# Order of the two heads of a pair in the matmuls of an RWKV-7 layer

## What is computed

```python
sa = einsum('bhij,bhj->bhi', s, at)
s = s * wt + sa[..., None] * bt + vt[..., None] * kt
y = einsum('bhij,bhj->bhi', s, rt)
```

## Time and profile before

| what | value |
|---|---|
| executions | 3149.65, 3150.62, 3152.99 us |
| span of the profiled execution (its own time; no other is given) | 3154.0 us |
| PE matmul busy | 2964.0 us (94%), 24726 instructions |
| PE weight load busy | 2386.1 us (76%) |
| DVE, ACT, POOL busy | 1796.9, 1140.6, 300.5 us |
| the slots of the RWKV layer | about 1140 to 1625 us |

### The profile page before, as it was taken

The page is one execution under the profiler, slowest core; times in us unless marked ns, Lnnn a source line. Parts: engine busy times, 40 slices in busy tenths (PEclk is TensorE's granted clock), DMA queues, the critical chain, the costliest instruction groups (busy, mean ns, idle before and its releaser), DMA issues. The chain is left out here.

```text
span 3154.0 us, 55883 instructions
## 1 busy us (share of the span) xinstructions
PE 2964.0 (94%) x24726; PEld 2386.1 (76%) x24726; DVE 1796.9 (57%) x2769; ACT 1140.6 (36%) x1779; POOL 300.5 (10%) x390
## 2 busy tenths in 40 slices
PE   7999998899998988898989999999899999999999
PEld 3775535899985468888949989876799897455898
DVE  3348566756554067778736555467555554465553
ACT  2236402434331234344223343444543433144432
POOL 2222011000000013323210000000000000200000
PEclk9999999999999999999989999999999999999999
DMA  7323544355543010000035545543355554423353
GB/s 263 104 107 107 187 149 146 117 188 192 191 172 120 27 28 3 3 3 3 32 132 177 190 161 179 180 156 134 100 168 181 165 178 174 139 75 132 109 187 134
DMA packets 258170, 409.33 MB, mean 130 GB/s; under 512 B 18647, under 2 KB 111208, under 8 KB 257800
## 3 DMA queue, kind: packets, MB, share of 16 engines
q1 hardware_dynamic: 253832, 392.50, 36.2%
q0 software_dynamic: 4096, 13.25, 1.5%
HBM read 400.68 MB, written 2.95 MB: 128 GB/s over the span
## 5 line engine op out<-in xcount | busy, mean ns | idle before, releaser
L353 DVE TENSOR_TENSOR ring_parts<-ring,arena_parts 128x2048 fp32r<-128x2048 f32 x270 | 598.4, 2256 | 285.7 <-ACT arena_parts L346 283.2
L346 ACT CAST arena_parts<-ring 128x2048 fp32r<-128x2048 f32 x270 | 495.4, 1885 | 517.1 <-PE psum L2822 229.5
L2822 PE MATMUL psum<-arena_parts 128*128 128x256 f32 x2816 | 514.6, 286 | 3.1 <-DVE arena_parts L578 2.1
L2822 PEld LDWEIGHTS psum<-arena_parts 128*128 128x128 f32 x2816 | 445.3, 195 | 4.2 <-DVE arena_parts L578 3.0
L2822 PE MATMUL psum<-arena_parts,ring_parts 128*128 128x256 f32 x1408 | 401.7, 285 | 0.0
L390 PE MATMUL psum<-arena_parts 128*128 128x512 f32 x1024 | 327.0, 393 | 2.0 <-DVE arena_parts L578 2.0
L2822 PEld LDWEIGHTS psum<-arena_parts,ring_parts 128*128 128x128 f32 x1408 | 274.0, 195 | 0.0
L1855 PE MATMUL psum<-arena_parts 128*128 128x512 f32 x768 | 236.6, 389 | 0.0
L390 PEld LDWEIGHTS psum<-arena_parts 128*128 128x128 f32 x1024 | 193.8, 190 | 43.0 <-DVE arena_parts L578 2.7
L390 PE MATMUL psum<-ring_parts,arena_parts 128*128 128x512 f32 x560 | 219.5, 392 | 0.0
L1840 PE MATMUL psum<-arena_parts 128*128 128x256 f32 x896 | 163.3, 285 | 4.2 <-DVE ring_parts L353 4.0
(11 more groups left out here) (498 smaller groups left out, 5888.1 us busy)
## 6 DMA issues: line engine op xcount, KB each, us to landing
ring<-in_mlp_w SPq DMA_DIRECT2D x48, 2048.0 KB, 8.2
ring<-in_ada_w SPq DMA_DIRECT2D x24, 2048.0 KB, 7.8
ring<-in_ffn_pre_w_gu SPq DMA_DIRECT2D x44, 1024.0 KB, 6.6
ring<-in_ffn_post_w_gu SPq DMA_DIRECT2D x44, 1024.0 KB, 7.1
ring<-in_ffn_pre_w_down SPq DMA_DIRECT2D x8, 2048.0 KB, 7.8
ring<-in_xmem_wkv SPq DMA_DIRECT2D x8, 2048.0 KB, 8.0
ring<-in_ffn_post_w_down SPq DMA_DIRECT2D x8, 2048.0 KB, 7.7
ring<-in_ab_w_in SPq DMA_DIRECT2D x7, 2048.0 KB, 7.7
```

Of the source, the lines that this page charges most:

```text
L346: nc.scalar.copy(high_view(name)[:, k, :], raw_view(name)[:, k, :]).then_inc(*up(act, ("high", name, h)))
L353: nc.vector.tensor_tensor(low_view(name)[:, k, :], raw_view(name)[:, k, :], high_view(name).bitcast(F32)[:, k, :], ALU.subtract)\
L2822: ins = nc.tensor.matmul(psum[:, b, 256 * j:256 * j + 256], s[:, k, at:at + P], x_parts[q][:, k, :], start=(k == 0 and i == 0), stop=(k == ...
```

## The change

Only the order of matmuls on PE changes, in three functions; shapes, banks, waits and counts stay.

```diff
             gram_pe, for f, z, c in gram_at(f, tick)
                 for r in HH:
                     k_, b_ = Kh[f % 2][z][r, s], Bh[f % 2][z][r, s]
                     if c < 4:
                         nc.tensor.matmul(psum[r, b, 0:64], b_, R_[f % 3][z][r, c, :], start=True, stop=True)
-                        nc.tensor.matmul(psum[r, b, 64:192].rearrange("p (a t) -> p a t", a=2), k_,
-                                         RA[f % 3][z][r, :, c, :], start=True, stop=True)
                     else:
                         nc.tensor.matmul(psum[r, b, 128:192], k_, A_[f % 3][z][r, c, :], start=True, stop=True)
-                    nc.tensor.matmul(psum[r, b, 192:256], b_, cst("eye64")[r, :], start=True, stop=True)
-                    ins = nc.tensor.matmul(psum[r, b, 256:320], k_, cst("eye64")[r, :], start=True, stop=True)
+                if c < 4:
+                    for r in HH:
+                        nc.tensor.matmul(psum[r, b, 64:192].rearrange("p (a t) -> p a t", a=2), Kh[f % 2][z][r, s],
+                                         RA[f % 3][z][r, :, c, :], start=True, stop=True)
+                for r in HH:
+                    nc.tensor.matmul(psum[r, b, 192:256], Bh[f % 2][z][r, s], cst("eye64")[r, :], start=True, stop=True)
+                for r in HH:
+                    ins = nc.tensor.matmul(psum[r, b, 256:320], Kh[f % 2][z][r, s], cst("eye64")[r, :],
+                                           start=True, stop=True)
             walk_pe: W
                     for r in HH:
                         if i:
                             nc.tensor.matmul(t[r], A_[f % 3][z][r, c, :], S[r, :], start=True, stop=False)
+                    for r in HH:
                         ins = nc.tensor.matmul(t[r], g_block(f, z, c, "KA")[r, :], VS[r, c, f, :],
             walk_pe: S
                             nc.tensor.matmul(t[r], g_block(f, z, c, "KT")[r, :], VS[r, c, f, :], start=True, stop=False)
+                        for r in HH:
                             ins = nc.tensor.matmul(t[r], g_block(f, z, c, "BT")[r, :], Ut[z][r, :], start=False, stop=True)
             walk_pe: Y
                         nc.tensor.matmul(t[r], R_[f % 3][z][r, c, :], S[r, :], start=True, stop=False)
+                    for r in HH:
                         nc.tensor.matmul(t[r], g_block(f, z, c, "KR")[r, :], VS[r, c, f, :], start=False, stop=False)
+                    for r in HH:
                         ins = nc.tensor.matmul(t[r], g_block(f, z, c, "BR")[r, :], Ut[z][r, :], start=False, stop=True)
             readout_pe
-            for h in HH:
-                for c in range(4):
+            for c in range(4):
+                for h in HH:
                     nc.tensor.matmul(psum[h, 4, 64 * c:64 * c + 64], Y[h, c, f, :], cst("eye64")[h, :],
                                      start=True, stop=True)
+                for h in HH:
                     ins = nc.tensor.matmul(psum[h, 4, 256 + 64 * c:320 + 64 * c], bonus[h, c, :],
```

## The result

The changed kernel takes 3134.77 us (median of 4, 3125.82 to 3136.51) against 3150.84 us before (4 runs on the same occasion), a ratio of 0.994 with an interval from 0.9926 to 0.9955: 16 us less, clear of the bound of 0.2%. The forecast was 3136.0.

A forecast was written before the change was run, and what follows sets the result against it. PE was taken to bound about half of each slot, DVE and ACT the rest. Slot savings summed to 18.0 us, less 3 for the clock: 15 off the median, 3136; range 3129 to 3146.

The forecast's parts named there:

- What bounds the slot: RWKV layer slot: PE bounds about half; the DVE and ACT parts keep their length and move forward with PE.
- Latent chunk: Eight passes a head: alternating takes 0.57 us instead of 0.74, saving 0.17, or 0.33 before an all-column matmul.
- Readout: Sixteen passes a head: alternating takes 0.93 us instead of 1.48, saving 0.55 a turn.
- The sum of a slot: The four slots with a readout and full preparation: 2.2 us saved each, 8.8 in all.
- The next slot: Slot after those four, no preparation left: all eight latent chunks count, plus a readout, 1.9 us saved.
- The one behind it: The following slot: the same 1.9 us saved.
- The last slot: Layer's final slot: 0.7 us at a readout, 4 × 0.12 at Y, 1.3 at the half-clock last readout; 2.5 saved.
- The clock: Shorter slots shift against half-clock stretches; good slots may lose 2.7 us each, bad ones gain; 3 us charged.
- rival A: Three or more slots hit longer low clock, or DVE chain binds: 3145 to 3148 us; 13 in 100 within, 1 slower.
- B, one bank: Neighbouring passes of different heads take turns at one PSUM bank: nearly 40 us slower, 3190; 4 in 100.
- C, time in the walk: Neighbours of one head cost time in W, S and Y too: some 35 us more saved, 3100; 3 in 100.
- head 1 is held by four passes: PE holds about four unrun passes of a head; n passes with head 0 first hold head 1 back n-4.

The follow-up runs named there:

- the clock held: Old and new order, each with additional unread matmuls before tick 2's S step and tick 9's W step for pairs 0 to 4: 3138.43 and 3117.22 us.
- two reorderings together: Kernel before, with the 128-column matmul last in latent chunks and the readout in blocks of four matmuls a head: 3141.54 us, ratio 0.9974.

## Why the prediction was right, point by point

- What bounds the slot: right. The stretch put down to PE is the one that shrank, from 21.70 to 19.20 us, and the DVE and ACT stretch behind it moved forward with its length: the 2.51 us are still there at the S step of tick 2.
- Latent chunk, 0.17 us each: right, 0.57 us measured. Before an all-column matmul 0.33 was forecast, 0.38 measured.
- Readout, 0.55 us a turn: 0.53 measured.
- W and S, nothing: right, by the timeline and by a kernel with this part alone (ratio 0.9999).
- The sum of a slot, 2.2 us: too small. With the clock held it is 57.01 - 54.32 = 2.7, and the layer 20.3 against my 18 (by the medians 18.9). Nearly all of it lies in the stretch that PE bounds (2.5 us), where I had counted 0.55 + 4 × 0.17 + 2 × 0.33 + 0.12 = 2.0. Of the other 0.5, 0.1 are the two chunks before an all-column matmul. Another 0.07 may be head 1's lag, carried from a latent chunk through S and Y up to L2237: that stretch takes 1.86 us (1327.53 to 1329.39) in place of 2.22 (1343.53 to 1345.75), 0.36 less, where 0.17 + 0.12 was counted. The rest are steps of some 0.05 us at other changes from one group to the next; their cause isn't shown.
- The next slot, 1.9 us: 3.0 measured (45.1 to 42.1), with the clock at 1.00 in both kernels, so that this one is the order's own.
- The one behind it, "the same": the term that failed in the plain change, 0.9 us lost (42.7 to 43.6). The wait for the projection's weights grew from 1.0 to 1.8 us, where I had put 0.3 at risk, and 6.8 us at half clock came with it, where before there was none. Without such a stretch the slot has 39.4 us in the new order, a wait of 0.5 us included, and 41.6 in the old: the order is worth 2.2 there too.
- The last slot, 2.5 us: right. The last two turns moved together by 1.3 us (25.2 to 23.9, 0.7 + 0.48 forecast), and from the last turn to the projection's next L2776 it is 3.54 us (1606.19 to 1609.73) in place of 4.85 (1625.39 to 1630.24), the 1.3 forecast. By the end of the layer 0.4 of that are left (36.2 to 35.8), with 23.4 us at half clock where before it was 19.5.
- The clock, charged at 3 us as one slot gone bad: the sign is right, the size open (2.8 by the medians, 5.7 or 9.3 by the layers), and the picture was wrong. Not one but all three good slots went bad, about 2.5 us each; the sign that I had named for rival A, slots of 58 us with a clock near 0.92, came about in each of them. The bad slot got no better by the clock: it had 10.2 us at half clock before and after, and gained 3.0 us by the order alone. What the clock gave back it gave before the first turn.
- Why the good slots went bad stays open. A longer wait alone doesn't explain it: the wait at tick 2 grew from 1.87 to 2.47 us, but in its slot of 60.9 us the kernel before has half clock behind that wait with the same 1.87. And the wait of W, with 6.8 us at half clock in place of 3.4, is 2.96 us in both.
- So the sum came out, 14.6 us on the layer by the profiles and 16 by the medians where 15 was forecast, in part by luck: what three slots and the one before the last gave up was made good by an order worth more than I had counted and by 7.1 us before the first turn, where my first two slots had 2.9. Of those, 3 are the clock's, since with the clock held that part gains 4.1, and another execution of the same kernel doesn't have them.
- The rivals. B, one bank: fell, two neighbouring passes of different heads take 0.058 us in one bank. C, time in the walk: fell with the kernel that changes the walk alone. A, given back: its mechanism was at work in three slots, at 7.5 us of the 8.1 that the order saves there, and its price of 8.1 was about right; the total stayed out of its range for the reasons just told. Its other half, a DVE chain that binds, fell at the held clock.
- That head 1 is held by four passes was right for the chunk and gave the number for the reordered chunk that doesn't alternate; the theory lacked the pass lost at each change of head.

## What to carry to other kernels

Matmuls of two heads on separate halves of the rows and columns ran side by side here only while both heads had instructions within reach: a block of up to four passes a head lost nothing, one of eight with long passes first lost 0.17 us of 0.74, one of sixteen 0.53 of 1.48. Alternate them, or put the short ones first. Before crediting a saving on PE, look at what the granted clock does behind its waits, stretch by stretch: here three slots gave back nearly all of 2.7 us each, and six matmuls that nobody reads, put into one wait a slot, were worth 13.5 us on top of the change's 16. And compare parts of the kernel, in more than one execution, before calling a total understood.

## What was not expected of the hardware

The slots keep near one length. Before the change three of them have 58.2 us; with the change, with the chunk products alone or with the wide matmul last, most have 57.9 to 58.0, though the PE work differs by up to 2.5 us; with two reorderings together they go 56.0, 59.8, 56.0, 59.9. With the clock held the lengths are 57.0 and 54.3. In the changed kernel the low stretches behind tick 2 begin at 1291.7, 1349.7, 1407.7 and 1465.7 us, 58.0 apart like the slots. So the low stretches, whose place against the slot's work and whose length change from kernel to kernel, seem to even out what the orders save; how they come to give nearly the same length each time, the runs don't show.
